# Layer 1 projections: small matmuls in column or row groups, the gate later, and the scaling of x moved from GpSimd to VectorE

## The reference

```python
xr, xw, xk, xv, xa, xg = [x + xx * mu[i] for i in range(6)]      # xx = x one frame earlier - x
r = xr @ w_r
w_log = -softplus(-(w0 + tanh(xw @ w_w1) @ w_w2)) - 0.5
k = xk @ w_k
v = xv @ w_v
a = sigmoid(a0 + (xa @ a1) @ a2)
g = sigmoid(xg @ g1) @ g2                                        # g1 is 1024 x 160
kk = heads(k * k_k)
kk = kk / maximum(sqrt(sum(square(kk), axis=-1)), 1e-12)         # the head squares and the norm
k = k * (1.0 + (a - 1.0) * k_a)
# ... the recurrence over the frames, a norm by head ...
bonus = sum(rh * kh * r_k, axis=-1) * vh
y = (y + bonus) * g @ w_o
```

## Time and profile before

| | |
|---|---|
| median of 3 runs | 1392.91 us (1391.98 to 1393.37) |
| profiled execution, its own time | 1387.37 us |
| its span, first to last instruction | 1385.6 us |
| mean granted TensorE clock | 0.992 |
| PE, DVE, ACT, POOL busy | 97%, 32%, 20%, 7% |
| DMA | 450.45 MB, mean 325 GB/s |

### The profile page before, as it was taken

How to read it: one execution, slowest core, us unless ns; L and a number is a source line. 1 busy time by engine, 2 the same in 40 slices (tenths; PEclk the granted TensorE clock), 3 DMA queues, 4 the chain that set the end, 5 groups by cost and what they waited for, 6 DMA issues and landing times.

```text
span 1385.6 us, 24728 instructions
## 1 busy us (share of the span) xinstructions
PE 1344.1 (97%) x10364; PEld 779.2 (56%) x10364; DVE 436.5 (32%) x982; ACT 271.4 (20%) x533; POOL 93.9 (7%) x124
## 2 busy tenths in 40 slices
PE   7999999999999999979999998999999999999997
PEld 6889443444434444339688998944444443434433
DVE  2245122222222222146652337622222222222213
ACT  1231211111111111112421331121111111111111
POOL 7202000000000000012003100300000000000001
PEclk9999999999999999999999999999999999999999
DMA  4697799999999999975323006679999999999993
GB/s 152 178 358 310 305 364 408 422 422 422 421 422 422 422 422 422 421 251 171 115 101 124 4 4 245 258 292 374 398 422 422 422 422 422 422 422 421 422 420 156
DMA packets 98666, 450.45 MB, mean 325 GB/s; under 512 B 16032, under 2 KB 45344, under 8 KB 48928
## 3 DMA queue, kind: packets, MB, share of 16 engines
q1 hardware_dynamic: 98592, 449.34, 80.9%
HBM read 448.26 MB, written 1.05 MB: 324 GB/s over the span
## 4 chain that ended last, share of the span: by engine, by line
PE 93%; DVE 5%; issue 1%; DMA 1%; ACT 1%; POOL 0%; SPq 0%; DVEq 0%; PEldq 0%; ACTq 0%
PE PS L1882 31%; PE PS L1921 17%; PE PS L1929 10%; PE PS L1853 7%; PE PS L549 4%; PE PS L512 3%; PE PS L1396 2%; PE PS L1373 2%; PE PS L1358 2%; PE PS L1901 1%; PE PS L1521 1%; PE PS L2002 1%; PE PS L1536 1%; PE PS L1545 1%; PE PS L1893 1%; PE PS L534 1%
## 5 line engine op out<-in xcount | busy, mean ns | idle before, releaser
L2234 DVE TENSOR_TENSOR y_parts<-PS,y_parts 128x512 fp32r<-128x512 f32 x128 | 88.5, 691 | 216.7 <-ACT y_parts L2136 216.7
L2208 DVE SCALAR_TENSOR_TENSOR AR<-AR,PS 128x256 f32<-128x256 f32 x64 | 30.8, 481 | 386.5 <-ACT AR L2114 386.5
L1929 PE MATMUL PS<-y_parts,token_map 128*128 128x512 f32 x496 | 146.6, 417 | 0.0
L1882 PE MATMUL PS<-AR,xT 128*64 128x512 f32 x512 | 115.7, 593 | 5.6 <-issue 5.5
L1929 PEld LDWEIGHTS PS<-y_parts,token_map 128*128 128x128 f32 x496 | 83.5, 188 | 60.9 <-issue 50.3
L1921 PE MATMUL PS<-AR 128*64 128x512 f32 x512 | 116.9, 598 | 0.0
L1921 PE MATMUL PS<-RING,AR 128*64 128x512 f32 x496 | 116.9, 598 | 0.0
L1882 PE MATMUL PS<-AR 128*64 128x512 f32 x512 | 115.5, 592 | 0.0
L2136 ACT CAST y_parts<-PS 128x512 fp32r<-128x512 f32 x128 | 75.0, 586 | 172.0 <-PE PS L1921 172.0
L1882 PE MATMUL PS<-RING,xT 128*64 128x512 f32 x480 | 108.1, 592 | 0.0
L1882 PE MATMUL PS<-RING,AR 128*64 128x512 f32 x480 | 108.1, 592 | 0.0
(11 more groups left out here) (315 smaller groups left out, 1575.7 us busy)
## 6 DMA issues: line engine op xcount, KB each, us to landing
RING<-in_moe_w_gate SPq DMA_DIRECT2D x64, 1024.0 KB, 11.8
RING<-in_moe_w_up SPq DMA_DIRECT2D x64, 1024.0 KB, 13.9
AR<-in_moe_w_gate SPq DMA_DIRECT2D x64, 1024.0 KB, 13.2
AR<-in_moe_w_up SPq DMA_DIRECT2D x64, 1024.0 KB, 15.2
AR<-in_moe_w_down SPq DMA_DIRECT2D x64, 1024.0 KB, 14.0
RING<-in_moe_w_down SPq DMA_DIRECT2D x62, 1024.0 KB, 15.1
AR<-in_ab_w_in SPq DMA_DIRECT2D x8, 1024.0 KB, 5.6
AR<-in_rw_w_o SPq DMA_DIRECT2D x4, 1024.0 KB, 5.3
```

Of the source, the lines that this page charges most:

```text
L1882: ins = nc.tensor.matmul(PS[s * B:(s + 1) * B, 4, :], gathered(k)[:, c:c + B], gate_and_up(slots[s])[:, k, :, :], start=(k == 0), stop=(k ...
L1929: ins = nc.tensor.matmul(PS[:, 2 * t + h, :], OHT[:, half, t, :], YS[:, n, h * 512:(h + 1) * 512], start=False, stop=True, skip_group_chec ...
L2208: nc.vector.scalar_tensor_tensor(out=HH[0:2 * B, :].rearrange("p (k j) -> p k j", k=FT), in0=by_row(SIL[0:2 * B, :]), scalar=GC[:, buf:buf ...
L2234: nc.vector.tensor_tensor(YS[:, 1, h * 512:(h + 1) * 512], PS[:, 5 + h, :], YS[:, 0, h * 512:(h + 1) * 512], ALU.subtract).then_inc(q["low ...
```

## The change

The scaling of X moves to VectorE, behind the input mixes of the low-rank layers, and runs before it waits for the keys. GpSimd now builds only WIN, a smaller OWN and a new matrix FOLD, as soon as the residual is done; the fourfold copy `g1b` is gone. The head squares, the bonus and the 32-column tail of the gate's first layer are matmuls of 32 output columns whose eight feature tiles go to four column groups in turn, two tiles summed in each. The norm is spread from four row groups of 32, so VectorE reads it in another pairing of tiles. The gate's tail is left as four partial sums; ScalarE copies them, one matmul with FOLD adds them and repeats them in all row groups. The bonus comes out with heads on rows and is copied and turned by two transposes. The gate's first layer stands behind all of the first two value chunks, and the values' function now does one tile, so that other work stands between tiles. The guard of the squares on VectorE stands ahead of the scaling of the keys.

```diff
@@ dve_mix1
+            v.wait_ge(s_gb, 32 * 2)
+            for t in range(TT):
+                v.wait_ge(s_za, t + 1)
+                v.wait_ge(s_zv, t + 1)
+                v.wait_ge(s_tr, 4 * 2 + 2 * t + 2)
+                link(V.tensor_tensor(X[:, t, :], X[:, t, :], GB[:, 0, :], ALU.mult))
+                link.sync()
+                V.tensor_tensor(X[:, t, :], X[:, t, :], GB[:, 1, :], ALU.add).then_inc(s_zg, 1)
             v.wait_ge(s_pj, TK + 8)
             for h in range(2):
                 mix(0, MR, range(4 * h, 4 * h + 4))
+            v.wait_ge(r["head_squares_done"], 1)
+            V.tensor_scalar(SSQ, PS[:, 1, 0:T], 1e-24, None, ALU.max).then_inc(r["head_squares_guarded"], 1)
             v.wait_ge(s_pe, 4 + TK + 8)
...
-            v.wait_ge(r["head_squares_done"], 1)
-            V.tensor_scalar(SSQ, PS[:, 1, 0:T], 1e-24, None, ALU.max).then_inc(r["head_squares_guarded"], 1)
@@ act_mix1
-            values(range(0, 2))
+            values(range(0, 4))
+            s.wait_ge(s_lh, 2)
+            A.copy(LH[:, 3, :], PS[:, 1, 0:T]).then_inc(s_lhc, 1)
             s.wait_ge(s_lh, 3)
             A.activation(LH[:, 2, :], PS[:, 0, 0:T], ACT.Sigmoid).then_inc(s_lhc, 1)
+            values(range(4, 5))
+            s.wait_ge(s_lh, 4)
             A.activation(LH[:, 3, :], PS[:, 1, 0:T], ACT.Sigmoid).then_inc(s_lhc, 1)
...
@@ gp_mix1
-            g.wait_ge(s_gb, 32 * 2)
-            for t in range(TT):
-                g.wait_ge(s_za, t + 1)
-                g.wait_ge(s_zv, t + 1)
-                g.wait_ge(s_tr, 4 * 2 + 2 * t + 2)
-                gp_scaled(link, t, slice(0, D))
-            link(G.memset(OWN, 1.0))
+            g.wait_ge(moe_shared["x_split"], TT)
+            g.wait_ge(s_res, 4 * TT)
             link(G.memset(WIN, 0.0))
             link.sync()
...
+            for rows in quarter_rows:
+                own = ident[rows, rows].rearrange("p (n a h) -> p n a h", n=8, a=2)[:, 0, :, :]
+                link(G.tensor_copy(OWN[rows, :, :, :], own.rearrange("p a (h o) -> p a h o", o=1).to_broadcast([32, 2, 2, HD])))
+                link(G.tensor_copy(FOLD[rows, :].rearrange("p (n c) -> p n c", n=4),
+                                   ident[rows, rows].rearrange("p (o c) -> p o c", o=1).to_broadcast([32, 4, 32])))
                 link.sync()
@@ pe_mix1
             for k in range(KT):
-                c0 = P - 2 - 2 * k
-                ins = mm(PS[:, 1, 0:T], WIN[:, c0:c0 + P], RT[:, k, :], start=(k == 0), stop=(k == KT - 1))
+                c0 = P - 2 - 2 * (k // 4)
+                ins = mm(PS[quarter_rows[k % 4], 1, 0:T], WIN[:, c0:c0 + 32], RT[:, k, :], start=(k < 4), stop=(k >= 4))
...
-                ins = mm(PS[:, k // 2, (k % 2) * T:(k % 2) * T + T], OWN[:, k * P:(k + 1) * P], SSQ, start=True, stop=True)
+                rows = quarter_rows[k % 4]
+                ins = mm(PS[:, k % 4, (k // 4) * T:(k // 4) * T + T], OWN[rows, k // 4, :, :].rearrange("p h d -> p (h d)"),
+                         SSQ[rows, :], start=True, stop=True)
...
-            values_chunk(0, XMIX[1])
+            for n in range(4):
+                values(n // 2, n % 2, XMIX[1])
             pe.wait_ge(s_lg, 16 * 6)
-            pe.wait_ge(r["gate_weights_copied"], 1)
             pe.wait_ge(s_xm, 10)
             pe.wait_ge(r["key_norm_used"], 1)
-            for n, w in enumerate((g1[:, :, 0:P], g1b.rearrange("p k o c -> p k (o c)"))):
-                for k in range(KT):
-                    ins = mm(PS[:, n, 0:T], w[:, k, :], XMIX[0][:, k, :], start=(k == 0), stop=(k == KT - 1))
-                ins.then_inc(s_lh, 1)
-            values_chunk(1, XMIX[1])
+            for k in range(KT):
+                ins = mm(PS[quarter_rows[k % 4], 1, 0:T], g1[:, k, P:160], XMIX[0][:, k, :], start=(k < 4), stop=(k >= 4))
+            ins.then_inc(s_lh, 1)
+            for k in range(KT):
+                ins = mm(PS[:, 0, 0:T], g1[:, k, 0:P], XMIX[0][:, k, :], start=(k == 0), stop=(k == KT - 1))
+            ins.then_inc(s_lh, 1)
+            values(2, 0, XMIX[1])
+            pe.wait_ge(s_lhc, 3)
+            mm(PS[:, 1, 0:T], FOLD, LH[:, 3, :], start=True, stop=True).then_inc(s_lh, 1)
             pe.wait_ge(r["bonus_terms_ready"], 1)
+            for k in range(KT):
+                c0 = P - 2 - 2 * (k // 4)
+                ins = mm(PS[quarter_rows[k % 4], 3, 0:T], WIN[:, c0:c0 + 32], T1[:, k, :], start=(k < 4), stop=(k >= 4))
+            ins.then_inc(r["bonus_done"], 1)
+            values(2, 1, XMIX[1])
+            pe.wait_ge(s_lhc, 6)
             for t in range(TT):
-                for k in range(KT):
-                    ins = mm(PS[:, 3, 16 * t + 2 * k:16 * t + 2 * k + 2], T1[:, k, t * P:(t + 1) * P], bones[:, 0:P:HD],
-                             start=True, stop=True)
-            ins.then_inc(r["bonus_done"], 1)
-            values_chunk(2, XMIX[1])
-            pe.wait_ge(s_lhc, 4)
+                ins = nc.tensor.transpose(PS[:, 2, t * P:(t + 1) * P], SSQ[:, t * P:(t + 1) * P], ident[:, :])
+            ins.then_inc(r["bonus_turned"], 1)
+            values(3, 0, XMIX[1])
```

More of the change, by code:

```diff
@@ L264, in program @@
         w2a2 = a1s(D)
-        g1b = a1s(KT, 4, 32)
+        FOLD = a1s(P)
         g2a = a1s(D)
@@ L274, in program @@
         gfl = GTT.rearrange("p k t -> p (k t)")
-        OWN, WIN = gfl[:, 0:D], gfl[:, D:D + 2 * P]
+        OWN, WIN = gfl[:, 0:2 * P].rearrange("p (a h d) -> p a h d", a=2, h=2), gfl[:, 2 * P:4 * P]
+        quarter_rows = [slice(32 * g, 32 * g + 32) for g in range(4)]
         area_a = Area(AR, l1x, AFL)
@@ L830, in program @@
                  "head_squares_guarded", "root_ready", "norm_ready", "norm_spread", "log_decay_ready", "key_norm_used",
-                 "keys_mixed", "decays_ready", "bonus_terms_ready", "bonus_done", "bonus_ready", "operands_ready",
-                 "norm_params_loaded", "low_ranks_out", "low_ranks_copied", "gate_weights_copied",
+                 "keys_mixed", "decays_ready", "bonus_terms_ready", "bonus_done", "bonus_turned", "bonus_ready", "operands_ready",
+                 "norm_params_loaded", "low_ranks_out", "low_ranks_copied",
                  "gate_out", "gram_done", "gram_masked", "unit_ready", "turned", "turned_copied",
@@ L1204, in act_mix1 @@
             receptance(range(6, 8))
-            values(range(0, 2))
+            values(range(0, 4))
+            s.wait_ge(s_lh, 2)
+            A.copy(LH[:, 3, :], PS[:, 1, 0:T]).then_inc(s_lhc, 1)
             s.wait_ge(s_lh, 3)
             A.activation(LH[:, 2, :], PS[:, 0, 0:T], ACT.Sigmoid).then_inc(s_lhc, 1)
+            values(range(4, 5))
+            s.wait_ge(s_lh, 4)
             A.activation(LH[:, 3, :], PS[:, 1, 0:T], ACT.Sigmoid).then_inc(s_lhc, 1)
-            values(range(2, 4))
             s.wait_ge(r["bonus_done"], 1)
-            A.copy(BONT[:, :, :].rearrange("p t h -> p (t h)"), PS[:, 3, 0:TT * 16]).then_inc(r["bonus_ready"], 1)
+            A.copy(SSQ, PS[:, 3, 0:T]).then_inc(s_lhc, 1)
+            values(range(5, 6))
+            s.wait_ge(r["bonus_turned"], 1)
+            for t in range(TT):
+                turned = PS[:, 2, t * P:(t + 1) * P].rearrange("p (g m) -> p g m", g=4)[:, :, 0:4]
+                ins = A.copy(BONT[:, t, :].rearrange("p (a g j) -> p g a j", a=2, g=4),
+                             turned.rearrange("p g (a j) -> p g a j", a=2))
+            ins.then_inc(r["bonus_ready"], 1)
+            values(range(6, 7))
             for n in range(4):
@@ L1214, in act_mix1 @@
                 A.copy(GTT[:, n::4, :], PS[:, n, :].rearrange("p (m t) -> p m t", m=2))
-            values(range(4, 8))
+            values(range(7, 8))
             s.wait_ge(s_pe, 4 + PROJECTED)
@@ L1360, in heads_chunk, with values @@
                     ins.then_inc(s_pj, 1)
-            def values_chunk(c, x):
+            def values(c, t, x):
                 pe.wait_ge(s_rw[c], RW0[c] + 16 * 3)
@@ L1366, in values_chunk @@
                 w = RWC[c].rearrange("p (k c) -> p k c", k=KT)
-                for t in range(TT):
-                    pe.wait_ge(s_pe, TV + 2 * c + t + 1)
-                    for h in range(2):
-                        for k in range(KT):
[L1371 to L1375, removed]
+                pe.wait_ge(s_pe, TV + 2 * c + t + 1)
+                for h in range(2):
+                    for k in range(KT):
+                        for q in range(2):
+                            n = t * P + (q ^ h) * CH
+                            ins = mm(heads_of(PS[half_rows[q], 4 + (2 * c + t) % 4, 0:CB])[:, :, h, :], x[:, k, n:n + CH],
+                                     heads_of(w[:, k, :])[:, :, h, :], start=(k == 0), stop=(k == KT - 1))
+                ins.then_inc(s_pj, 1)
             def low_ranks(half):
@@ L1450, in pe_mix1 @@
             pe.wait_ge(s_xm, 9)
-            values_chunk(0, XMIX[1])
+            for n in range(4):
+                values(n // 2, n % 2, XMIX[1])
             pe.wait_ge(s_lg, 16 * 6)
```

(26 more changed lines are left out.)

9 lines of the change are left out of this document (1 added, 8 removed).

## The result

| | before | after |
|---|---|---|
| timed with the prediction, median (lowest to highest, runs) | 1392.45 us (1388.9 to 1393.37, 4) | 1372.5 us (1369.36 to 1379.47, 4) |
| ratio of those | | 0.9868, 95% interval 0.9827 to 0.991 |
| timed again later, median | 1389.33 us (1385.63 to 1398.16, 17) | 1376.15 us (1370.93 to 1379.72, 6) |
| ratio of those | | 0.9899, 95% interval 0.9877 to 0.9922 |
| profiled execution, its own time | 1387.37 us | 1369.36 us |

The change made the kernel faster. The first comparison says 18.4 us (0.0132 of 1392.45), the second, with more runs, 14.0 (0.0101 of 1389.33, interval 10.8 to 17.1). Forecast was 12.1.

A forecast was written before the change was run, and what follows sets the result against it. TensorE, with 93% of the span, was taken to bound the kernel; gains 3.3 + 2.6 + 0.3 + 2.0 + 2.3 + 1.6 = 12.1 us gave 1380.8 us, range 1377.5 to 1385.5.

The forecast's parts named there:

- The same difference on 1392.91: Run median assumed to stand 5.5 us above the profiled execution's time, as before, giving 1380.8 us.
- x off GpSimd, to the keys: VectorE's input work before the keys no longer held by GpSimd's scaling: gain 2.4 us (1.7 to 3.2).
- clock at the keys' start: Low clock when TensorE resumes: between nothing and 2 us could come back, nothing taken.
- head squares: Sixteen records in four column groups take 1.07 us instead of 3.67: gain 2.6.
- wait for the receptance weights: Load issued after x is scaled lands late: new wait between 0 and 2.0 us, 1.7 taken.
- norm spread: L1446 takes the four-group form, 1.07 us instead of 3.67: gain 2.6.
- gate's wait, gate, bonus, clock behind it: Gate's wait gone 0.3 us, gate's first layer 2.0, bonus 2.3, no clock fall behind the bonus 1.6.
- Start: Before the keys: GpSimd's new copies meet VectorE's input work, costing between nothing and 1.5 us, 0.8 taken.
- my two bounds: First receptance load lands 9.0 us after its own issue, or 16.1 after the first issue in the queue.
- serial groups: Column groups one by one, 3.67 us each; squares lose 2.6, of which 1.7 covered: gain 6.0, chance 0.04.
- Clock behind the bonus: Value chunk behind the two-column bonus ran at low clock; with full-width streams no fall expected: gain 1.6 us.
- Rivals 1 to 4: Weights in time, 0.17; column groups not four abreast, 0.12; wait for weights drops clock, 0.08; sparse tiles hold clock low, 0.03.

The follow-up runs named there:

- bonus_two_columns: Changed kernel with the bonus again as 32 records of two columns, without the copy and the transposes: 1381.34 us, ratio 0.9947.
- squares_wide: Changed kernel with the head squares again over 128 output rows, eight matmuls summed one after another: 1376.23 us, ratio 0.9906.
- gate_early: Changed kernel with the gate's first layer again behind two value tiles, ScalarE's copies in the same order: 1377.63 us, ratio 0.9927.

## Why the prediction was right or wrong

**The forecast time was wrong, by a step that the sum did not price.** "The gate's second layer, the recurrence and the experts keep their instructions and shift as a whole": they keep them, but not their durations, and the same holds for the work ahead. In the ten profiled executions (two of each kernel and six of variants) the residual is done between 613.8 and 619.1 us, the keys' stretch takes 30.9 to 33.1, the recurrence 97.6 to 100.6 and the part behind it 540.4 to 544.2. The residual, the keys and the end have no order by kernel: the changed kernel has both 613.8 and 619.1. "The same difference on 1392.91" and a range built only from the unknown costs of the change put this at nothing. It is nearly as large as the miss of 8.3 us: the four-run medians differ by 20.0 us, those of 17 and 6 runs by 13.2, since the first series has the kernel before 3.1 higher and the changed kernel 3.7 lower. The longer series puts the gain nearer the forecast than the first result was: 14.0 us (10.8 to 17.1) against 12.1.

A small part of the rest is not chance and was missed too. The first 31 us of the recurrence, up to its first eight transposes (start us, us, line, tiles, form, count; before, then after), take 31.06 and 31.04 in the two executions of the kernel before, 30.82 in bonus_two_columns and 30.36 or 30.37 in the seven others:

```profile
776.59 1.09 PE L1555 MATMUL PS<-ident,AR 128*128 128x128 f32 x8
759.68 1.09 PE L1576 MATMUL PS<-ident,AR 128*128 128x128 f32 x8
```

So 0.7 us of the recurrence's difference goes with the kernel, though its instructions are the same; no run shows why. What comes behind it, 67.3 to 69.8 us, has no such order.

**Term by term**, first profile against first profile:

| term | forecast | measured |
|---|---|---|
| x off GpSimd, to the keys | 2.4 | 2.9 |
| clock at the keys' start | 0 | 0.5 |
| head squares | 2.6 | 2.6 |
| wait for the receptance weights | -1.7 | -1.4 |
| norm spread | 2.6 | 2.6 |
| gate's wait, gate, bonus, clock behind it | 6.2 | 5.9 |
| sum, residual to recurrence | 12.1 | 13.2 |

The 0.5 of the clock is luck of this pair: the keys' stretch takes 31.5 and 31.2 in the two executions of the kernel before, 31.0 and 33.1 in those of the changed one. The terms that repeat add up to 12.6.

*Start.* The term was right in kind and mis-sized by the collision with the head maps: 0.8 assumed, 0.3 measured by moving them. The time in which the two meet was not what was off: the copies run from 613.84 to 617.72, 3.9 us behind the residual, inside the 2.4 to 4.2 that the forecast allowed, and overlap VectorE's input work from 615.88 on for 1.8 us. In that time its four-element instruction took 0.27 and its four mixes 1.35, where the next ones took 0.16 and 1.14: short copies hold it for far less than the two long ones of the kernel before did.

*The load that waits for x* was seen: the place, and 1.3 to 1.4 us where 1.7 was forecast. Of my two bounds the landing stood nearer the upper: 11.1 us after issue, 15.3 after the first issue, where I had 16.1. That it covers part of the squares' gain was said for serial groups, and squares_wide showed it.

*Column groups* run four abreast: 1.04 to 1.07 for sixteen records of 128*32, as in row groups. The Trainium skill's 3.07 for four row tiles and 2.38 for three column tiles (TensorE: Matmul & The Clock Gate, Part 3) are below the 3.67 / 1.04 = 3.5 that four column tiles reach here. A change of tiling mode opens no gap: 64 records of receptance (L1371) take 6.96 us from start to start ahead of a group of the same tiles and 7.01 to 7.06 ahead of one of others, so a change costs at most 0.1.

*Gate and bonus.* Fold 0.63 instead of 0.46 and transposes 0.37 instead of 0.26; they are short groups whose last record's own length counts. The rest is as forecast, and gate_early confirmed the wait that the move avoids (2.73, where the text has 2.6 on top of 0.3). The norm spread and the gate's tail were not undone by themselves; their 2.6 and 1.8 are read from the profiles.

*Clock behind the bonus.* Right in cause. It fell at the end of the two-column stream in all three profiled executions that had it and, at this place, in none of the seven others; its price is not fixed: 1.6, 1.3 and 2.7 in value tiles.

Rivals 1 to 4 did not come about: the weights were late, the groups ran together, the wait of 1.3 did not bring the clock down, and the sparse tiles did not hold it low.

**What stays open.** Why the pause at the end of the experts varies from 0.5 to 3.4 us, why the recurrence does by 3 and why 0.7 of that goes with the kernel was not settled. Part of the recurrence's difference is one or two gaps of 0.4 to 0.8 us on TensorE, 82 to 88 us into it, that the profile calls issue; the first execution of the changed kernel, whose recurrence is the shortest, has none of them.

## What to carry to other kernels

Sum a change's terms against one profile, but take the width of the range from how much executions of the kernel before differ in the stages that the change does not touch; where only three times are shown, that is more than their spread. When work moves to another engine, follow the semaphore that it raises: a load queue that waited for it can turn part of the gain into a new wait, and putting the urgent loads ahead of it lengthened no stage here. Reductions with few output columns did better here in column groups with the long side streaming, which saved both their time and the clock behind them.

## What the runs showed that was not expected

Four column groups of 32 with full 128-row inputs reach 3.5 times the serial rate (3.67 against 1.04 us). With a stream of 32 two-column records (3.7 to 4.0 us) the granted clock fell from 1.00 to 0.50 in three of three executions, although TensorE counts as busy throughout. Twelve executions of one kernel differed by up to 12 us (1383.49 to 1395.39). TensorE's pause before the residual ran from 0.5 to 3.4 us between executions, and the matmuls behind it ran at a granted clock of 1.00 in the four with 0.5 to 1.4 and fell to 0.50 in the six with 2.0 to 3.4.
